# Modulation rows added up four to a tile in a two-block transformer kernel

## What is computed

```python
# first block: for each of 2 layers, 9 pieces of 1024 (layer 0 also for the context vector)
m  = (silu(c)     @ w_mod[i] + b_mod[i]).reshape(b, 1, 9, d)
mc = (silu(c_ctx) @ w_mod[i] + b_mod[i]).reshape(1, 1, 9, d)
x  = x + 0.5 * gate * swiglu(rms_norm(x, g) * (1 + scale) + shift, w13, w2)
# second block: for each of 2 layers, 6 pieces of 1024
mod = silu(c_2) @ ada_w[layer] + ada_b[layer]
```

## Time and profile before

| | |
|---|---|
| median of 3 runs | 2502.81 us (2500.32 to 2507.3) |
| the profiled execution: its own time | 2501.64 us |
| its span in the trace | 2499.8 us |
| mean granted TensorE clock | 0.958 |
| PE busy | 2397.4 us (96%) |
| DVE busy | 1430.5 us (57%) |
| ACT busy | 1000.5 us (40%) |
| moved by DMA | 535.45 MB, mean 214 GB/s |

### The profile page before, as it was taken

The page is one execution under the profiler, slowest core; times in us unless marked ns, Lnnn a source line. Parts: engine busy times, 40 slices in busy tenths (PEclk is TensorE's granted clock), DMA queues, the critical chain, the costliest instruction groups (busy, mean ns, idle before and its releaser), DMA issues.

```text
span 2499.8 us, 35746 instructions
## 1 busy us (share of the span) xinstructions
PE 2397.4 (96%) x15358; PEld 2158.7 (86%) x15358; DVE 1430.5 (57%) x1609; ACT 1000.5 (40%) x1257; POOL 4.5 (0%) x12
## 2 busy tenths in 40 slices
PE   9999999989999999999999988899999899899997
PEld 7788888867998999888998986899998888899996
DVE  0875676323763465234652442688887433888886
ACT  2211132214330332042321323577776344676774
POOL 0000000000000000000000000000000000000000
PEclk8999999989999999999999988899999789899998
DMA  7456767522777477543775431488886332488884
GB/s 277 172 196 240 265 227 271 192 68 79 259 279 277 171 292 294 186 152 129 262 276 212 151 118 37 148 300 294 300 305 242 142 121 75 179 304 295 296 307 180
DMA packets 94195, 535.45 MB, mean 214 GB/s; under 512 B 9984, under 2 KB 12296, under 8 KB 46800
## 3 DMA queue, kind: packets, MB, share of 16 engines
q1 hardware_dynamic: 92480, 524.33, 58.3%
q0 software_dynamic: 816, 5.65, 0.6%
q10 hardware_dynamic: 736, 3.10, 0.3%
HBM read 531.97 MB, written 1.06 MB: 213 GB/s over the span
## 4 chain that ended last, share of the span: by engine, by line
PE 90%; DVE 6%; ACT 3%; issue 1%; DVEq 0%; ACTq 0%
PE PS L777 25%; PE PS L1231 12%; PE PS L850 9%; PE PS L888 8%; PE PS L1259 7%; PE PS L812 5%; PE PS L935 5%; DVE moe_low L2202 2%; PE PS L1199 2%; PE PS L733 2%; PE PS L699 2%; PE PS L1179 1%; PE PS L659 1%; PE PS L742 1%; PE PS L876 1%
## 5 line engine op out<-in xcount | busy, mean ns | idle before, releaser
L777 PE MATMUL PS<-h_parts,ring_low 128*128 128x256 f32 (+1 forms) x1408 | 440.0, 313 | 0.0
L777 PE MATMUL PS<-h_parts,g_parts 128*128 128x256 f32 x2112 | 383.0, 284 | 0.9 <-DVE h_parts L1813 0.9
L2202 DVE TENSOR_TENSOR moe_low<-moe_ring,W_HIGH 128x2048 fp32r<-128x2048 f32 x128 | 292.9, 2290 | 83.1 <-ACT W_HIGH L1615 83.1
L777 PEld LDWEIGHTS PS<-h_parts,g_parts 128*128 128x128 f32 x2112 | 328.9, 192 | 2.4 <-issue 1.2
L1231 PE MATMUL PS<-moe_low,HXH 128*96 128x256 f32 x1024 | 287.9, 281 | 0.0
L777 PEld LDWEIGHTS PS<-h_parts,ring_low 128*128 128x128 f32 x1408 | 269.9, 192 | 16.1
L1615 ACT ACTIVATE W_HIGH<-moe_ring 128x2048 fp32r<-128x2048 f32 x128 | 244.5, 1912 | 23.4 <-PE PS L1259 22.7
L850 PE MATMUL PS<-G,ring 128*128 128x256 f32 x1056 | 236.5, 385 | 2.8 <-DVE G L1898 2.8
L850 PEld LDWEIGHTS PS<-G,ring 128*128 128x128 f32 x1056 | 201.3, 192 | 30.7 <-DVE G L1898 3.4
L1460 ACT ACTIVATE SG<-PS 128x256 f32<-128x256 f32 (+1 forms) x88 | 38.4, 437 | 462.9 <-PE PS L777 462.9
L1231 PEld LDWEIGHTS PS<-moe_low,HXH 128*96 128x96 f32 x1024 | 166.2, 162 | 0.3
(11 more groups left out here) (316 smaller groups left out, 4653.6 us busy)
## 6 DMA issues: line engine op xcount, KB each, us to landing
moe_ring<-moe_w SPq DMA_DIRECT2D x192, 1024.0 KB, 4.9
CB<-mod_rows SPq DMA_DIRECT2D x200, 512.0 KB, 5.9
ring<-up_w SPq DMA_DIRECT2D x88, 1024.0 KB, 5.0
ring<-lin_w SPq DMA_DIRECT2D x55, 1024.0 KB, 4.9
ring<-down_w SPq DMA_DIRECT2D x24, 1408.0 KB, 6.0
CB<-mod_dual SPq DMA_DIRECT2D x24, 512.0 KB, 4.1
ring<-down_w SPq DMA_DIRECT2D x10, 1024.0 KB, 7.8
ring<-mod_w SPq DMA_DIRECT2D x8, 1024.0 KB, 7.0
```

Of the source, the lines that this page charges most:

```text
L777: return mm(dst(h), a[:, k, h * P:(h + 1) * P], b[:, k, :], start=start, stop=(k == KT - 1 and j == 2), skip_group_check=True)
L2202: tt(by_tile(moe_low[:, moe_slot(l, p), :]), by_tile(moe_ring[:, moe_slot(l, p), :]), w_high_tiles(p), ALU.subtract).then_inc(w_low, 1)
```

## The change

Rows are grouped by four. A chunk is still 128 partitions x 1024, but it now holds 32 input positions of each of four rows: partition 4i+j holds input i of row j. VectorE does the same one multiply-add for each chunk with a scalar for each partition. After 32 chunks one accumulator holds the partial sums of four rows, interleaved by partition, and eight products with a stationary piece of 128 x 128 and a moving operand of four columns (`block`: column j is 1 where the partition number modulo 4 is j) give the sums of all four rows.

- The 28 rows make 7 groups of 32 chunks: still 224 chunks. Group 0 is the three dual rows with the first single row; it alone is added twice (two accumulators, now 32 dual chunks in place of 24), and has 16 products. The others have 8 each.
- A chunk of groups 1 to 6 is one DMA whose source takes 32 rows of 4 KB from each of four places 4 MB apart. A chunk of group 0 is four DMAs of 32 partitions each, to every fourth partition.
- One accumulator (`roots`) serves groups 1 to 6; the first chunk of a group waits for the column sums of the group before (`colsum_done`), and the plan has a unit without chunks there. The accumulators in `CAT` and `H`, and with them ScalarE's wait for six sums ahead of one copy in `down0`, are gone.
- `take_group` files four rows in one instruction (32 columns), for group 0 in two, and waits for its own end.
- The plan changes: feed-forward 0 has 104 chunks (112 before), feed-forwards 1 and 2 have 40 as before, feed-forward 3 has 40 (32 before).
- `down0` waits for one group ahead of it and for three groups ahead of the next norm's sums (for 11 rows before). The take of the dual rows in unit 12 goes.
- At the start GpSimd issues four small DMAs that spread the conditioning columns in the new layout (`cond_raw`), and ScalarE waits for them (`ld_cond`) before one SiLU on 128 x 128 and before its first norm. Two SiLU instructions go.

```diff
-                src = mod_dual[n] if n < N_DUAL_CHUNKS else mod_rows[n - N_DUAL_CHUNKS]
+                g, k, part = n // GROUP_CHUNKS, n % GROUP_CHUNKS // ROWS, slice(n % ROWS * PARTS, (n % ROWS + 1) * PARTS)
                 if n >= 4:
                     sp.wait_ge(acc_steps, steps_after(n - 4))
+                if g == 0:
+                    for j in range(ROWS):
+                        src = mod_dual[j * KT + k, part, :] if j < N_DUAL else mod_rows[k, part, :]
+                        put(ROWS_W[j::ROWS, n % 4, :], src)
+                else:
+                    r0 = (ROWS * (g - 1) + 1) * KT + k
+                    src = bass.AP(mod_rows.tensor, (r0 * P + part.start) * D, [[D, PARTS], [KT * P * D, ROWS], [1, D]])
+                    put(ROWS_W[:, n % 4, :], src)
...
-                for d in range(KT):
-                    last = mm(PS[:, ROW_BANK[r], d:d + 1], ACC[ROW_ACC[r]][:, d * P:(d + 1) * P], tab("ones")[:, 0:1],
-                              start=True, stop=True)
+                for j in range(1 if g else 2):
+                    acc = ACC if g else DUAL_ACC[:, j, :]
+                    for d in range(KT):
+                        at = j * ROWS * KT + d
+                        last = mm(PS[:, GROUP_BANK[g], at:at + 3 * KT + 1:KT], acc[:, d * P:(d + 1) * P],
+                                  tab("block")[:, 0:ROWS], start=True, stop=True)
...
 CHUNKS_AT = (
-    ([3] * 8 + [4] * 9 + [3] * 4 + [0], [4] * 5 + [2] + [4, 2] + [4] * 3 + [0]),
-    ([1, 1, 2] * 6 + [1, 1, 0, 0], [3, 2, 3, 2, 2, 2, 0, 0]),
-    ([1, 1, 2] * 6 + [1, 1, 0, 0], [3, 2, 3, 2, 2, 2, 0, 0]),
-    ([1] * 20 + [0, 0], [2] * 6 + [0, 0]),
+    ([3] * 10 + [2] + [4] * 8 + [0, 4, 0], [4] * 5 + [2, 4, 2, 0, 4, 4, 0]),
+    ([1, 1, 2] * 6 + [0, 1, 1, 0], [3, 3, 2, 2, 2, 2, 0, 0]),
+    ([2, 1] * 5 + [1, 0] + [1, 2] * 4 + [1, 0], [2] * 5 + [1, 0, 0]),
+    ([1] * 8 + [0] + [1, 2] * 6 + [0], [3, 3, 2, 2, 2, 2, 0, 0]),
 )
...
+            act.wait_ge(ld_cond, 64)
+            af(cond_rows[:, :, :], cond_raw[:, :, :], ACT.Silu).then_inc(cond_ready, 1)
...
+            for part in range(ROWS):
+                src = bass.AP(cols_in.tensor, part * PARTS * NCOLS, [[NCOLS, PARTS], [0, ROWS], [1, 4 * KT]])
+                pool.dma_start(cond_raw[:, part, :], src).then_inc(ld_cond, 16)
```

More of the change, by code:

```diff
@@ L84, in chunk_plan @@
         counts = list(ups_at) + list(downs_at)
-        steps = [dict(chunks=[], sums=[], dual=[], takes=[]) for _ in counts]
+        steps = [dict(chunks=[], sums=[], takes=[]) for _ in counts]
         for i, count in enumerate(counts):
@@ L88, in chunk_plan @@
                 steps[i]["chunks"].append(n)
[L89 to L95, removed]
+                if n % GROUP_CHUNKS == GROUP_CHUNKS - 1:
+                    steps[i + 1]["sums"].append(n // GROUP_CHUNKS)
+                    steps[i + 2]["takes"].append(n // GROUP_CHUNKS)
                 n += 1
         plan.append(steps)
-    assert n == (N_DUAL + N_ROWS) * KT
+    assert n == N_GROUPS * GROUP_CHUNKS
     return plan
@@ L210, in tables @@
     t["zeros"] = np.zeros((P, P))
+    t["block"] = (i[:, None] % ROWS == np.arange(8)[None, :])
     t["w4"] = np.tile([4.0, 3.0, 2.0, 1.0], (P, 2))
@@ L690, in first_mods, with column_sums @@
                 spread_roots(0)
[L692 to L697, removed]
-                for d in range(KT):
-                    last = mm(PS[:, ROW_BANK[r], d:d + 1], ACC[ROW_ACC[r]][:, d * P:(d + 1) * P], tab("ones")[:, 0:1],
-                              start=True, stop=True)
-                last.then_inc(colsum_done, 1)
[L703 to L708, removed]
-                        last = mm(PS[:, 6, at:at + 1], DUAL_ACC[:, r % 2, j, d * P:(d + 1) * P], tab("ones")[:, 0:1],
-                                  start=True, stop=True)
-                last.then_inc(dual_summed, 1)
+            def column_sums(g):
+                pe.wait_ge(acc_steps, steps_after((g + 1) * GROUP_CHUNKS - 1))
+                wait(pe, rows_taken, g)
+                for j in range(1 if g else 2):
[4 more added lines that the diff above has]
+                                  tab("block")[:, 0:ROWS], start=True, stop=True)
+                last.then_inc(colsum_done, 1)
             def sums(f, i):
-                for r in PLAN[f][i]["dual"]:
-                    dual_column_sums(r)
-                for r in PLAN[f][i]["sums"]:
-                    column_sums(r)
+                for g in PLAN[f][i]["sums"]:
+                    column_sums(g)
             def h_arrived(n, k):
@@ L1880, in take_row @@
[L1880 to L1884 removed]
+                for j in range(1 if g else 2):
+                    acc = ACC if g else DUAL_ACC[:, j, :]
+                    at = 4 * (m // ROWS) + (group_cond(g) if g else j)
+                    c = cond_rows[:, m % ROWS, at:at + 1]
+                    if m == 0:
+                        if g > 1:
+                            dve.wait_ge(colsum_done, g)
+                        ts(acc, w, c, None, ALU.mult).then_inc(acc_steps, 1)
+                    else:
+                        dve.wait_ge(acc_steps, steps_after(n - 1) if g else 2 * n - 1 + j)
+                        stt(out=acc, in0=w, scalar=c, in1=acc, op0=ALU.mult, op1=ALU.add).then_inc(acc_steps, 1)
@@ new lines, in take_group @@
+            def take_group(g):
+                dve.wait_ge(colsum_done, g + 1)
+                at = ROW_TILE0 + (g * ROWS - N_DUAL) * KT
+                bias = COL["mod_b"].start + at
+                if g == 0:
+                    line(tt(M[:, at:at + N_DUAL * KT, 1], PS[:, GROUP_BANK[0], ROWS * KT:(ROWS + N_DUAL) * KT],
+                            cols[:, bias:bias + N_DUAL * KT], ALU.add))
+                tt(M[:, at:at + ROWS * KT, 0], PS[:, GROUP_BANK[g], 0:ROWS * KT], cols[:, bias:bias + ROWS * KT], ALU.add)\
+                    .then_inc(rows_taken, 1)
+                dve.wait_ge(rows_taken, g + 1)
+                line.wait()
@@ L1898, in up @@
                     tt(G[:, i, 0:N], SG[:, i % 4, 0:N], src, ALU.mult).then_inc(g_ready, 1)
-                    for r in step["takes"]:
-                        take_row(r)
+                    for g in step["takes"]:
+                        take_group(g)
                     for n in step["chunks"]:
```

94 lines of the change are left out of this document (31 added, 63 removed).

## The result

The median went from 2505.06 us (four runs, 2500.32 to 2509.52) to 2446.54 us (four runs, 2445.27 to 2450.48): ratio 0.977, interval 0.975 to 0.979. The profiled execution took 2446.25 us with a span of 2444.4 us, where that of before had 2499.8 us. The forecast was 2457 us, the range 2450 to 2468. Three kinds of things stand in those 10 us: a pace of the products that no step of the prediction had, a clock gain sized too small, and small costs sized at nothing. The experiments take them one after the other.

A forecast was written before the change was run, and what follows sets the result against it. TensorE, 90% of the span with the column sums in it, was taken as the bound. Gains of 40.4 (sums), 4.7 (clock) and 0.3 us (a wait) made 45.4, from 2501.6 to 2456.2, stated as 2457 us; range 2450 to 2468.

The forecast's parts named there:

- The sums: Column sums on TensorE: 248 products in 54.09 us become 64 in 13.66 us; gain 40.4 us.
- rival 5: Column sums: a four-column product costs double, +13.4 us, 2470 us; chance 0.03.
- rival 2: Scattered chunks come at half rate in units with four chunks: +18 us, 2475 us; chance 0.06.
- Rival 4: Chunks become the bound in units with four chunks, slower than before: +185 us, some 2640 us; chance 0.03.
- The start: ScalarE's wait for four small DMAs before the first norm's squares: some 13 us of cover, cost 0.
- The clock: Falls of TensorE's clock behind blocks of sums: 6.97 us lost before, one 2.3 us fall left, gain 4.7 us.
- slow block: Second dual block of column sums in feed-forward 0, at a lower clock: 4.49 us against 3.47, 1.02 us.
- The end of `down0`: Norm's 32 small sums with a fall of the clock; whether the fall goes was open: 0, at most 3.4 us.
- two in six: Blocks of sums in `down`: two of six were followed by a fall, so none was taken after.
- Rival 1: The clock doesn't follow the sums; falls stay in number and only change places: 2462 us; chance 0.14.
- two of the three: Long dual blocks of sums in feed-forward 0: two of three were followed by a fall of the clock.
- Rival 3: Cover too short in the ten dual units, VectorE or SP late: +11 us, 2468 us; chance 0.06.

The follow-up runs named there:

- the kernel with the pad: Changed kernel with another 8 unused columns behind `block`, moving the tiles over the late tables 32 bytes further; 2455.14 us, ratio 0.979.
- fourfold: Changed kernel with each four-column product of the column sums written as four of one column, 256 products for 64; 2528.18 us, ratio 1.008.
- wide products: Changed kernel with three extra 128-column products into a spare bank ahead of each four-column one, except in group 2; 2488.53 us, ratio 0.994.
- before_w0: Kernel before with only `W0_HIGH` and `G0_HIGH0` moved by 32 bytes to a multiple of 64, `H0_LOW` left in place; 2502.74 us, ratio 0.999.
- the other plan: Changed kernel with another chunk table: dual chunks thinned, one chunk per `up` unit in feed-forwards 2 and 3, more in `down`; 2440.84 us, ratio 0.975.

## Why the prediction was right where it was, and wrong where it was not

**The sums: right.** 128 records in seven blocks of the predicted lengths, 13.7 us in place of 54.1: 40.4 us, nearly three quarters of the whole. The step that carried it, a product costs the same with four moving columns as with one, held (0.21 us), so rival 5 is out. That the weight load sets this price is argued from PEld being busy throughout, and no run isolates it. The one microsecond of the block at the lower clock counts in it.

**What was costed at nothing, and cost nothing.** The scattered chunks (rivals 2 and 4): chunks of groups 1 to 6 and the four DMAs of group 0 in the trace of after, with the median from issue to landing last,

```profile
CB<-mod_rows SPq DMA_DIRECT2D x68, 512.0 KB, 5.2
...
CB<-mod_dual SPq DMA_DIRECT2D x81, 128.0 KB, 2.6
```

in 200 to 420 us and 66 to 178 us. The same stretch of before has 5.1 us, so four places 4 MB apart cost nothing when 32 neighbouring rows are read in each. The rule of the Trainium skill that stood beside rival 2 (DMA: Bandwidth & Descriptors) doesn't reach this pattern. Rival 4, the one on the slower side, is out with it. TensorE waits for no chunk and no SP. The start: the first norm's squares run from 15.32 us, where they ran from 15.61.

```profile
13.70 0.31 ACT L1715 ACTIVATE cond_rows<-cond_raw 128x128 f32<-128x128 f32 x1 [6.41 <-DMA cond_raw<-cols_in]
14.03 1.28 ACT L1377 ACT_TABLE_LOAD   x1
15.32 4.27 ACT L1389 ACTIVATE G<-X 128x512 f32<-128x512 f32 x8
```

ScalarE does wait 6.41 us for the four small DMAs, but they are there by 13.7 us. The wait of 0.31 us at the end of `down0` went, as predicted.

**The missing step: the pace of the products.** The prediction said "units of feed-forward 0 of 11.2 us back to back"; they are of 10.88 us. It went through what each edit removes, adds and moves in time, and not through what it moves in memory: `block` is a table like the others, placed ahead of buffers that TensorE reads. Nothing in the trace of before pointed to it, and the edit did, since addresses in this kernel are worked out from the table's columns. Its size: 0.32 us in each of 21 units of `up(0)` is 6.7, less what VectorE's cover took back 5.4 us, measured against the kernel with the pad, and with 2 to 3 us in `down0` some 8 us together. This term by itself puts the result outside the range: with it undone, 2455.1 us is inside.

**The clock: the mechanism right, the size too small.** The terms for falls in the feed-forwards came to 5.7 us (4.7, and 1.0 in the slow block). The falls lost 11.9 us before and 3.4 after, so 8.5 went. Two choices failed and one went the other way. The end of `down0` was kept at nothing, with 3.4 us as the bound; its fall went entirely, 3.4. The fall behind group 0 cost 1.7, not 2.3. And the one block left in a `down` has a fall behind it (11.29 us again), where two in six had spoken for none: +1.7. The prediction's reading of the earlier trace rows, that blocks of one-column sums bring the clock down with TensorE busy, is what the kernels with fourfold and with wide products confirm. Rival 1 (falls stay in number) is out. But which block gets a fall isn't settled by its length: 1.7 us ones in `up` never had one, the 3.47 us one of after in each of four traces. The trace that the prediction had was the exception in "two of the three": in the second trace of before and in the three of its variants all three long blocks are followed by a fall. In `down` it is two of six in four of these five traces, and none in the fifth (before_w0).

**Rival 3 in small.** "Such periods follow each other ten times now" was costed at nothing because 1.13 us were over in each. The quicker products took 0.32 of that, and in six of the units the cover ran out by up to 0.3 us: weight loads waited 1.8 us in all, and the intervals between `SG`s grew by 1.3. With the pad in the kernel after, where units are of 11.20 us, there is no such loss: every interval from 80.23 to 203.43 us is 11.20. So by its own numbers the step was right, and the missing pace undid it: the timeline of DVE in after shows 0.82 us over, where before had 1.13.

```profile
98.79 2.28 DVE L1846 TENSOR_TENSOR ring_low<-ring,W_HIGH 128x2048 fp32r<-128x2048 f32 x1
101.89 0.69 DVE L1898 TENSOR_TENSOR G<-SG,PS 128x512 f32<-128x512 f32 x1 [0.82 <-ACT SG L1466]
```

**A misread row.** "At most two in a unit of `up` of 11.6 us (34.87/3)" took x288 for three units. It is six, of 5.8 us, since a unit on 256 columns is 48 products of half the width. In a unit of 5.76 us VectorE has product, split and two chunks, 0.42 + 2.29 + 2.67 us by its rows, and little is over; so the units with two chunks are longer by 0.22 us. The change has nine more of them (21 for 12). Of the 12, six stood beside a block of sums and were no longer for it; of the 21 only two. So 19 intervals are longer for 6: 13 x 0.22 = 2.9 us that the prediction had at nothing. The same 11.6 us stands in rival 2, where chunks at half rate would have had far less room in those feed-forwards than it says. The kernel with the other plan shows the cost and takes most of it away.

**Behind the change.** Mixer C takes 2.1 us longer in four of the five traces with the plan of after (not with fourfold products, where all before it lasts longer), and not with the other plan; its falls cost 6.8 us there against 5.1. Why wasn't isolated. Everything behind the first products of mixer E, where no instruction differs, takes 4.7 us less, and about that much less of it is at the lower clock. It varies between executions of the same kernel: 961.2 and 963.4 us in two of before, 956.5 and 957.8 in two of after. The five traces of before and its variants lie between 958.1 and 963.5, the six of after and its variants between 956.5 and 960.9, so most of it seems to come with the change, though the two ranges overlap; why is open.

**The sum again**, in spans: -45.4 (forecast) -8 (pace) -2.8 (clock in the feed-forwards) +2.9 (units with two chunks) +2.1 (mixer C) -4.7 (the rest of the program) +0.8 (the start, and mixer E up to the products of L944) = -55.1, against -55.4 measured. The waits for `ring_low` in `up(0)` are inside the -8.

## What to carry to other kernels

Follow an edit through memory as through time: any buffer that grows shifts those placed behind it, and here 32 bytes were worth some 8 us, more than any step of the prediction but the sums themselves. Blocks of products with few moving columns can cost twice, by their number (0.21 us each, whatever the columns) and by the clock that falls behind some of them, so merging them can pay more than their own length. Before saying that something is hidden, count the units in the row (x288 at 48 a unit) and ask what the cover is once the engine beside it gets quicker. A gap of TensorE in the chain isn't yet a wait of TensorE: look at its own timeline.

## What the runs showed of the hardware that was not expected

- TensorE's fp32r products of 128 x 128 on 512 columns took 0.2267 us each, in the mean over a unit's 48, with all operands at multiples of 64 bytes. They took 0.2333 us with the weights' high parts and the activations' low part 32 bytes off (16 of the 48 read both, 16 the weights alone, 16 neither): 3% of the pace, without exception in the nine kernels of this study. With one of the two buffers off it was 0.231 (weights aligned, 11.09 us for 48, and not beside dual chunks) and 0.232 (activations aligned, 11.13).
- A fp32 product with four moving columns took 0.21 us, like one with one column; one with 128 columns added 0.22 us.
- The granted clock fell to 0.50 behind blocks of narrow products with PE busy 1.00 throughout: 1.7 us lost behind 3.47 us of them, 12.0 in and behind a block of 64 of them that took 23.1 us; and not at all in or behind 14.2 us of narrow and 128-column products mixed.
- 32 rows of 4 KB from each of four places 4 MB apart landed in 5.2 us for 512 KB, as 128 neighbouring rows did (5.1).
